# First block of a two-block transformer kernel: three feed-forward pieces kept for the last accumulation, the last transposes moved behind its first products, and ScalarE applying the next block's norm

## The chip, the cores and the metric

The kernel runs on one core of a Trainium2 chip. The metric is the device time of one execution in microseconds (us), the median of several runs; lower is better. TensorE (PE) multiplies matrices, VectorE (DVE) and ScalarE (ACT) work element by element, GpSimd (POOL) does small column arithmetic here, and SyncE (SP) issues the weight loads. Each engine works through its own instructions in their order and meets the others only at semaphores, so an instruction that waits holds up all that stand behind it on its engine.

## What is computed

256 rows of width 1024 pass through a first block of two layers and then a second block of two layers. The change touches the end of both layers of the first block and the first norm of the second. Cut to that part:

```python
for i in range(2):                                   # first block
    ...                                              # attention, gating, w_o, layer norm 1
    gate, up = jnp.split(x @ w_ffn_in[i], 2, axis=-1)          # 1024 -> 2 x 2816
    ffn = (jax.nn.silu(gate) * up) @ w_ffn_out[i]              # 2816 -> 1024
    ple = (p[i] @ w_ple[i]) * jax.nn.sigmoid(x @ w_ple_gate[i])
    x = layer_norm(ALPHA * x + ffn + ple, ln2_g[i], ln2_b[i])
for layer in range(2):                               # second block
    h = modulate(rms_norm(x, norm_mix[layer]), sh1, sc1)       # x*rsqrt(mean(x^2)+eps), then scale and shift
    ...                                              # h @ w_in, attention, w_out, squared-relu MLP
```

## The kernel before

The rows are two tiles of 128 (`t` is 0 or 1). Every float32 product is made of three: each operand is split in a high and a low part, and high x high, high x low and low x high are added up in PSUM. So a weight piece ("item", at most 128x2048) is loaded by SP into `RAW`, its high part written to `WB` by ACT (`high`, L1737; in the trace every activation has line L1732), and its low part by DVE (`low`, L1939). The activations are split likewise: `XTH`/`XTL` for x transposed, `HTH`/`HTL` for the feed-forward's middle.

The order of the work is written out by one Python pass: `do(part, ...)` appends to a list, and each engine's program then walks through that list. `advance` issues high and low parts for at most three items ahead of the products (`cur["pairs"]`); `plan` gives the order of the weights in memory, which is the order of loads and of use.

The feed-forward runs over 11 pieces of 256 columns. For piece `c` PE makes two items of `w_ffn_in` (24 products of 512 columns each), ACT applies silu (`ffn`, L1868), DVE multiplies into `GB` (L2268). `ffn_turn` transposes a piece on PE (4 products of 128 columns, L1631); ACT then writes `HTH` and DVE `HTL` (L2022). Only then can the piece be multiplied with its item of `w_ffn_out` (24 products, `partial`), which accumulates in four PSUM banks, one for each tile `t` and half `c` of the 1024 output columns. Pieces 0 to 8 are multiplied as soon as they are transposed. Pieces 9 and 10 are kept for one last call of `partial`, which goes bank by bank in the order (t,c) = (0,0), (0,1), (1,0), (1,1), so that the first rows can be finished while the last are still being multiplied.

`last` follows each bank: DVE adds it to `X` (L2276) and makes the statistics of half a row (L2229). After the second half of a tile come the aggregate (L2234), POOL's reciprocal root (`rsqrt`, L1527 and L1529), and DVE's `ln_scale` (L2240) and `ln_shift` (L2248), which leaves the layer's result in `X`. In layer 0 that tile is transposed straight into `XTH`/`XTL`. In layer 1 the second block's norm stands between: ACT squares and sums the row (`norm_sq`, L1884), POOL makes the root, DVE multiplies into `MIX` (`norm_apply`, L2253), PE transposes (`modulate`), ACT scales and shifts half the columns and writes `XTH`, DVE does the other half and `XTL` (L2040, L2046). `go(0, pad=14)` is the call that does this for tile 0; `pad` is a number of products without use (L1584) that PE makes ahead of the transposes.

Then `linear2` multiplies with `even_w_in_2`: for tile 0 the items 139 and 140 (128x1536 each), the transposes of tile 1, item 141 (128x1152), and then the same items for tile 1.

Of the kernel before, what the change touches and what calls it, by code (L numbers as in the profile page):

```python
# [13 lines left out]
ACT = mybir.ActivationFunctionType  # L14
# [32 lines left out]
def plan():  # L47
# [12 lines left out]
    for i in range(2):  # L60

        all_rows("w_in", i, 1024, (768, 1092), (1604, 2116), (0, 384), (384, 768), (1092, 1604))
        all_rows("w_ple", i, 256, halves[0])
        all_rows("w_o", i, 1024, *halves)
        all_rows("w_ple", i, 256, halves[1])
        all_rows("w_ple_gate", i, 1024, *halves)
        for c in range(12):
            if c < 11:
                all_rows("w_ffn_in", i, 1024, [(c * 256, c * 256 + 256), (DFF + c * 256, DFF + c * 256 + 256)])
            if 1 <= c <= 8:  # L70
                ada(*ADA[i * 8 + c - 1])
            if c:
                out.append(("w_ffn_out", i, (c * 256 - 256, c * 256), [(0, 1024)]))
    for i in range(2):
# [110 lines left out]
def program(nc, W, xd, xTd, pTd, posd, pos2d, colvd, cstd, cstbd, vecd, sgwd, smalld, condd, out):  # L185
    with ExitStack() as ctx:
# [83 lines left out]
        def do(part, *args):  # L270
            order.append((part, args))
# [3 lines left out]
        def take():  # L275
            return free.pop(0)
# [231 lines left out]

        def partial(name, parts, ps, first, last, evac=None):
            its = []  # L510
# [14 lines left out]
            if evac is None:  # L525
                for n in range(len(its)):
                    advance()
                    one(n, 0)
                    one(n, 1)
            else:  # L530
                assert len(its) <= cur["pairs"]
                advance()

                for t in range(2):
                    for c in range(2):
                        for n in range(len(its)):
                            one(n, t, (c,))
                        evac(t, c, ("mm", (g, t, c)))
                advance()
# [225 lines left out]

        def norm_sums(t, after):
            g = uid()
            ss = col(1)
            do("norm_sq", g, t, ss, after)
            do("rsqrt", ("nt", g), ss, 1.0 / D, 1e-6, ("norm_sq", g))  # L770

            def apply():
                do("norm_apply", g, t, ss)
                hn[t] = ("hn", g)
            return apply

        def norm_tile(t, after):
            norm_sums(t, after)()

# [20 lines left out]
        for i in range(2):  # L800
# [185 lines left out]
            ht_free = [list(t_pe), list(t_pe)]  # L986
            acc4 = None
            for c in range(12):
# [6 lines left out]
                if c:  # L995
                    d = c - 1
                    r2 = 2 * (d % 4)
                    b, fr = take()
                    g = uid()
                    do("ffn_turn", g, [GB[:, t, (d % 2) * 256 + kt * 128:(d % 2) * 256 + kt * 128 + 128]  # L1000
                                       for kt in range(2) for t in range(2)], r2, b,
                       [("ffn", (i, d, t)) for t in range(2)] + fr, ht_free[d % 2])
                    give(b, ("tl", g))
                    f_free[d % 2] = [("tp", g)]
                if c < 11:
                    run(gen)
                if c:
                    if acc4 is None:
                        acc4 = [[take(), take()], [take(), take()]]
                    part_ = (r2, [("tl", g)])  # L1010
                    if d < 9:
                        ht_free[d % 2] = [partial("w_ffn_out", [part_], acc4, d == 0, False)]
                    elif d == 9:
                        part9 = part_
            x_o, x_n = x_w, [None, None]
# [11 lines left out]
            def last(t, c, done):  # L1027
                do("add_out", (i, t, c), t, c, acc4[t][c][0], [done] + x_o[t])
                give(acc4[t][c][0], ("add_out", (i, t, c)))
                ln_half((i, 2, t), t, c, ("add_out", (i, t, c)))  # L1030
                if c == 0:
                    return

# [4 lines left out]

                before = norm_sums(0, x_n[0]) if t and i else None
                x_n[t] = ln_tile((i, 2, t), t, between, before, (lambda: go(0, pad=14)) if t and i else None)  # L1040
                if t and i:
                    advance(1)
                if t and i == 1:
                    norm_tile(1, x_n[1])

            t_pe = [partial("w_ffn_out", [part9, part_], acc4, False, True, last)]
            pt_free = list(t_pe)
# [681 lines left out]
        def scalar_program(eng):  # L1729
# [154 lines left out]
            def norm_sq(g, t, ss, after):  # L1884
                for e in after:
                    on.wait_ge(*at(*e))
                act(MIX[:, t, :], X[:, t, :], ACT.Square, accum_out=ss).then_inc(*up("norm_sq", g))

            def lambdas(lt, _):
                on.wait_ge(*at("lam_dot", 0))  # L1890
                act(lt, lt, ACT.Exp).then_inc(*up("lam_exp", 0))
# [24 lines left out]
            def diff_out(t, b, r, _, __, op, after):  # L1916
# [3 lines left out]
                for e in after:  # L1920
# [4 lines left out]
                         modulate=modulate, hin=hin, lat=lat, gelu=gelu, sel_score=sel_score, sgu_ln=sgu_ln,  # L1925
                         p_split=p_split, soft=soft, ple=ple, gate=gate, ffn=ffn, relu2=relu2, norm_sq=norm_sq,
                         lambdas=lambdas, lat_sq=lat_sq, mla_k=mla_k, qk_sq=qk_sq, gain=gain, diff_out=diff_out)
# [541 lines left out]
```

## Time and profile before

| | us |
|---|---|
| median of 3 runs | 1319.9 (1319.08 to 1319.96) |
| the profiled execution, its own time | 1320.38 |
| its span, first to last instruction | 1318.6 |
| PE busy | 1279.9 (97%) |
| DVE busy | 912.1 (69%) |
| ACT busy | 659.2 (50%) |
| POOL busy | 110.9 (8%) |
| mean granted clock of PE | 0.994 |

Times in the rows below are microseconds from the span's start, of that one profiled execution. The 3% in which PE is not busy is made of many waits of about one microsecond.

### The profile page before, as it was taken

What the parts mean: (1) busy time and instruction counts of PE and PEld (TensorE: products, weight loads), DVE (VectorE), ACT (ScalarE), POOL (GpSimd) and SP (SyncE); (2) the same over time, 40 slices, a digit from 0 to 9 for tenths busy, and PEclk for the clock granted to TensorE, in tenths of its full rate; (3) what the DMA queues carried; (4) which work ended last, traced back from release to release, by engine and by line L of the source; (5) the groups of instructions that cost most, each with busy time, mean ns of one, the idle gap of its engine ahead of it and who ended that gap; (6) DMA issues with size and microseconds to landing.
All of it is one profiled execution on the core that took longest, in us unless ns stands there. A gap on an engine that the chain in (4) does not pass through costs nothing.

```text
span 1318.6 us, 15858 instructions
## 1 busy us (share of the span) xinstructions
PE 1279.9 (97%) x6336; PEld 1058.8 (80%) x6336; DVE 912.1 (69%) x1223; ACT 659.2 (50%) x888; POOL 110.9 (8%) x145
## 2 busy tenths in 40 slices
PE   8999999999999999999999899999999979999998
PEld 6878888887878888888699787888887867888886
DVE  6968777766787777775768857857567775744444
ACT  6645433443563543344475646545446654745442
POOL 2002000000000100000225200000004320000000
PEclk9999999999999999999999999999999989999999
DMA  9616678873643678886264305876765420555450
GB/s 376 248 65 234 238 302 309 306 290 132 224 152 114 228 265 312 303 307 226 67 211 145 112 10 215 314 292 256 287 223 191 160 96 32 194 189 192 170 181 32
DMA packets 41113, 270.35 MB, mean 205 GB/s; under 512 B 4656, under 2 KB 4672, under 8 KB 12880
## 3 DMA queue, kind: packets, MB, share of 16 engines
q1 hardware_dynamic: 38288, 259.83, 53.4%
q0 software_dynamic: 2464, 8.98, 1.8%
q8 instruction: 50, 0.82, 0.2%
q10 hardware_dynamic: 288, 0.52, 0.1%
q14 instruction: 23, 0.19, 0.0%
HBM read 268.27 MB, written 1.05 MB: 204 GB/s over the span
## 4 chain that ended last, share of the span: by engine, by line
PE 79%; DVE 12%; ACT 5%; issue 2%; POOL 1%; DMA 0%; DVEq 0%; ACTq 0%; POOLq 0%
PE ps L1617 48%; PE ps L1607 24%; PE ps L1631 4%; DVE WB L1939 3%; PE ps L1719 2%; ACT WB L1732 1%; ACT E L1732 1%; DVE st L2155 1%; PE ps L1694 1%; DVE SCR L2057 1%; POOL st L1529 1%; DVE SCR L2058 1%; ACT XTH L1732 0%; DMA GB<-xTd 0%; DVE st L2308 0%
## 5 line engine op out<-in xcount | busy, mean ns | idle before, releaser
L1939 DVE TENSOR_TENSOR WB<-RAW,WB 128x2048 fp32r<-128x2048 f32 (+3 forms) x211 | 453.2, 2151 | 239.3 <-ACT WB L1732 238.9
L1732 ACT ACTIVATE WB<-RAW 128x2048 fp32r<-128x2048 f32 (+3 forms) x211 | 379.8, 1802 | 206.2 <-PE ps L1617 202.5
L1607 PE MATMUL ps<-WB,XTH 128*128 128x512 f32 (+3 forms) x1176 | 312.5, 387 | 6.2 <-ACT XTH L1732 4.1
L1617 PE MATMUL ps<-WB,XTH 128*128 128x512 f32 (+3 forms) x1176 | 304.6, 380 | 4.8 <-DVE WB L1939 4.7
L1617 PE MATMUL ps<-WB,XTL 128*128 128x512 f32 (+3 forms) x1176 | 303.9, 380 | 1.9 <-DVE XTL L2046 1.4
L1617 PEld LDWEIGHTS ps<-WB,XTH 128*128 128x128 f32 x1176 | 217.4, 189 | 47.1 <-DVE WB L1939 9.0
L1617 PEld LDWEIGHTS ps<-WB,XTL 128*128 128x128 f32 x1176 | 218.3, 189 | 41.3 <-DVE XTL L2046 2.3
L1607 PEld LDWEIGHTS ps<-WB,XTH 128*128 128x128 f32 x1176 | 212.8, 189 | 44.4 <-ACT XTH L1732 7.2
L1607 PE MATMUL ps<-WB,HTH 128*128 128x512 f32 (+1 forms) x452 | 126.9, 396 | 0.6 <-ACT HTH L1732 0.5
L1617 PE MATMUL ps<-WB,HTH 128*128 128x512 f32 (+1 forms) x452 | 126.5, 395 | 0.0
L1617 PE MATMUL ps<-WB,HTL 128*128 128x512 f32 (+1 forms) x452 | 126.4, 394 | 0.0
L2001 DVE CUSTOM_DVE_ANT_0 RAW<-RAW,cond,colv 128x1024 f32<-128x1024 f32 x96 | 119.3, 1280 | 0.0
L1527 POOL TENSOR_SCALAR st<-st 128x1 f32<-128x1 f32 (+2 forms) x40 | 27.5, 688 | 909.2 <-DVE st L2234 518.3
L1617 PEld LDWEIGHTS ps<-WB,HTH 128*128 128x128 f32 x452 | 84.9, 188 | 20.3
L1732 ACT ACTIVATE HTH<-ps 128x512 fp32r<-128x512 f32 (+1 forms) x58 | 32.0, 587 | 138.3 <-PE ps L1631 138.1
L1617 PEld LDWEIGHTS ps<-WB,HTL 128*128 128x128 f32 x452 | 85.0, 188 | 20.0
L1607 PEld LDWEIGHTS ps<-WB,HTH 128*128 128x128 f32 x452 | 84.6, 188 | 20.6 <-ACT HTH L1732 1.0
L1732 ACT ACTIVATE GB<-ps 128x256 f32<-128x256 f32 (+1 forms) x86 | 41.9, 488 | 91.9 <-PE ps L1617 91.9
L1732 ACT ACTIVATE E<-ps,st 128x128 f32<-128x128 f32 (+1 forms) x104 | 46.8, 458 | 66.7 <-DVE st L2171 38.9
L2022 DVE TENSOR_TENSOR HTL<-ps,HTH 128x512 fp32r<-128x512 f32 x54 | 35.7, 685 | 31.9 <-ACT HTH L1732 31.9
L1529 POOL TENSOR_TENSOR st<-st,cst 128x1 f32<-128x1 f32 (+2 forms) x40 | 51.1, 1278 | 3.3
L1732 ACT ACTIVATE H<-ps 128x384 f32<-128x384 f32 (+2 forms) x48 | 24.5, 534 | 26.8 <-PE ps L1617 26.5
(183 smaller groups left out, 948.8 us busy)
## 6 DMA issues: line engine op xcount, KB each, us to landing
RAW<-W SPq DMA_DIRECT2D x220, 1024.0 KB, 4.9
RAW<-W SPq DMA_DIRECT2D x22, 768.0 KB, 4.5
VEC<-vecd POOLq DMA_DIRECT2D x10, 512.0 KB, 5.6
RAW<-W SPq DMA_DIRECT2D x8, 512.0 KB, 3.6
RAW<-W SPq DMA_DIRECT2D x4, 576.0 KB, 3.8
RAW<-W SPq DMA_DIRECT2D x2, 648.0 KB, 3.9
T<-sgwd POOLq DMA_DIRECT2D x2, 512.0 KB, 8.5
X<-xd SPq DMA_DIRECT2D x1, 1024.0 KB, 18.5
```

Source lines behind the costliest of these rows:

```text
L1527: eng.tensor_scalar(x, x, scale, eps, ALU.mult, ALU.add).then_inc(*own.up())
L1529: eng.tensor_tensor(x, x, MH.to_broadcast([128, x.shape[1]]), ALU.pow).then_inc(*up("rsqrt", key))
L1607: eng.matmul(banks[b][:, 0:cw], x2[j][0], hi[:, j, c0:c0 + cw], start=first and j == 0, stop=False)
L1617: op = eng.matmul(banks[b][:, 0:cw], x2[j][0 if low_w else 1], (lo if low_w else hi)[:, j, c0:c0 + cw], start=False, stop=last and end and ...
L1631: op = eng.transpose(banks[b][0:rows, j * 128:j * 128 + 128], src, ident)
L1694: eng.matmul(banks[b][:, c:c + nk], q, ks, start=n == 0, stop=True, skip_group_check=True)
L1719: op = eng.matmul(banks[b][:, c0:c0 + dv], PET[:, u["i"], blk * 128:blk * 128 + 128], val, start=(j == 0), stop=(j == len(lst) - 1))
L1732: return eng.activation(dst, src, f, **k)
L1939: eng.tensor_tensor(WB[:, it["raw"], 0:w], RAW[:, it["raw"], 0:w], WB[:, it["high"], 0:w].bitcast(F32), ALU.subtract).then_inc(*up("wl", n))
L2001: op = eng.tensor_tensor_reduce(view[:, q, :], view[:, q, :], cond[:, :], 1.0, colv[:, b0:b0 + 1], ALU.mult, ALU.add, modc[:, it["layer"], ...
L2022: eng.tensor_tensor(HTL[:, r2:r2 + 2, :], banks[b][:, :].rearrange("p (n q) -> p n q", n=2), HTH[:, r2:r2 + 2, :].bitcast(F32), ALU.subtra ...
L2057: eng.tensor_tensor(P4, x4, cb, ALU.mult).then_inc(*own.up())
```

## The change

`plan` and the loop over the pieces now keep pieces 8, 9 and 10 for the last call of `partial`; piece 8 is no longer multiplied between the `w_ffn_in` items. Piece 10 is transposed inside that call, through `turn_last`, after piece 8's products for bank (0,0). For tile 1 piece 8's products are made for both halves first. In layer 1 the norm of both tiles is applied by ACT (`norm_apply_a`), tile 0's as soon as its layer norm is done; `go(0)` comes right behind the last bank with `pad=6`, and the layer norm of tile 1 comes behind it.

```diff
@@ plan
-            if c:
-                out.append(("w_ffn_out", i, (c * 256 - 256, c * 256), [(0, 1024)]))
+            for d in range(8 if c == 10 else c - 1, c) if c and c != 9 else ():
+                out.append(("w_ffn_out", i, (d * 256, d * 256 + 256), [(0, 1024)]))
@@ partial
                 for t in range(2):
                     for c in range(2):
                         for n in range(len(its)):
+                            if turn_last and t and n == 0:
+                                if c == 0:
+                                    one(0, 1)
+                                    advance(1)
+                                continue
                             one(n, t, (c,))
+                            if turn_last and (t, c, n) == (0, 0, 0):
+                                turn_last()
                         evac(t, c, ("mm", (g, t, c)))
@@ norm_sums(t, after, by="norm_apply"), norm_tile(t, after, by="norm_apply")
-                do("norm_apply", g, t, ss)
+                do(by, g, t, ss)
@@ the loop over the pieces
-                    if d < 9:
+                    if d < 8:
                         ht_free[d % 2] = [partial("w_ffn_out", [part_], acc4, d == 0, False)]
-                    elif d == 9:
-                        part9 = part_
+                    else:
+                        kept.append(part_)
@@ last
                 if c == 0:
+                    if t and i:
+                        norm_tile(0, x_n[0], "norm_apply_a")
                     return
...
-                before = norm_sums(0, x_n[0]) if t and i else None
-                x_n[t] = ln_tile((i, 2, t), t, between, before, (lambda: go(0, pad=14)) if t and i else None)
+                if t and i:
+                    go(0, pad=6)
+                x_n[t] = ln_tile((i, 2, t), t, between)
                 if t and i:
                     advance(1)
-                if t and i == 1:
-                    norm_tile(1, x_n[1])
-            t_pe = [partial("w_ffn_out", [part9, part_], acc4, False, True, last)]
+                    norm_tile(1, x_n[1], "norm_apply_a")
+            t_pe = [partial("w_ffn_out", kept, acc4, False, True, last, lambda d=d, r2=r2, g=g: turn_ffn(d, r2, g))]
@@ scalar_program
+            def norm_apply_a(g, t, ss):
+                on.wait_ge(*at("rsqrt", ("nt", g)))
+                act(MIX[:, t, :], X[:, t, :], ACT.Copy, scale=ss).then_inc(*up("hn", g))
```

What this does to the engines' orders, at three places. On PE, at the end of the loop over the pieces (either layer; `cst,GB` are the transposes, HTH and HTL the feed-forward's middle), there stood before:

```order
L1617 MATMUL ps<-WB,XTH 128x512 x4
L1631 MATMUL ps<-cst,GB 128x128 x4
L1607 MATMUL ps<-WB,HTH 128x512 x2
L1617 MATMUL ps<-WB,HTH 128x512 x2
L1617 MATMUL ps<-WB,HTL 128x512 x2
```

and now stands:

```order
L1632 MATMUL ps<-WB,XTH 128x512 x4
L1622 MATMUL ps<-WB,HTH 128x512 x2
L1632 MATMUL ps<-WB,HTH 128x512 x2
L1632 MATMUL ps<-WB,HTL 128x512 x2
L1646 MATMUL ps<-cst,GB 128x128 x4
L1622 MATMUL ps<-WB,HTH 128x512 x2
```

Six products of piece 8 now stand ahead of the transposes of piece 10; piece 9's follow, and piece 10's are the third six.

On ACT, in layer 1 from the last silu (`GB<-ps`) to the first norm, before:

```order
L1732 ACTIVATE WB<-RAW 128x2048
L1732 ACTIVATE GB<-ps 128x256 x2
L1732 ACTIVATE HTH<-ps 128x512
L1732 ACT_TABLE_LOAD
L1732 ACTIVATE st<-st 128x2
L1732 ACTIVATE WB<-RAW 128x1536
L1732 ACTIVATE MIX,st<-X 128x1024
L1732 ACTIVATE GB<-ps,modc 128x128 x4
```

and now:

```order
L1747 ACTIVATE GB<-ps 128x256 x2
L1747 ACT_TABLE_LOAD
L1747 ACTIVATE st<-st 128x2
L1747 ACTIVATE WB<-RAW 128x2048
L1747 ACTIVATE HTH<-ps 128x512
L1747 ACTIVATE WB<-RAW 128x1536
L1747 ACTIVATE MIX,st<-X 128x1024
L1747 ACTIVATE MIX<-X,st 128x1024
L1747 ACTIVATE GB<-ps,modc 128x128 x4
```

The high part of piece 10's weights (128x2048) moved behind the last silu, since three items are already ahead, and with the table load it stands ahead of `HTH`; layer 0 has the same order without the table load and the small exponential. The norm's multiplication (`MIX<-X,st`) is new on ACT.

On DVE, in layer 1 from the last bank's addition to `X`, before:

```order
L2276 TENSOR_TENSOR X<-X,ps 128x512
L2229 BN_STATS st<-X 128x6
L2234 BN_AGGR st<-st 128x2
L2253 TENSOR_SCALAR MIX<-X,st 128x1024
L2240 SCALAR_TENSOR_TENSOR X<-X,st,VEC 128x1024
L2040 TENSOR_SCALAR GB<-ps,modc 128x128 x4
L2046 TENSOR_TENSOR XTL<-GB,XTH 128x4x128 x2
L2248 SCALAR_TENSOR_TENSOR X<-X,st,VEC 128x1024
L1939 TENSOR_TENSOR WB<-RAW,WB 128x1536
```

and now:

```order
L2295 TENSOR_TENSOR X<-X,ps 128x512
L2248 BN_STATS st<-X 128x6
L2059 TENSOR_SCALAR GB<-ps,modc 128x128 x4
L2065 TENSOR_TENSOR XTL<-GB,XTH 128x4x128 x2
L2253 BN_AGGR st<-st 128x2
L2259 SCALAR_TENSOR_TENSOR X<-X,st,VEC 128x1024
L2267 SCALAR_TENSOR_TENSOR X<-X,st,VEC 128x1024
L1958 TENSOR_TENSOR WB<-RAW,WB 128x1536
```

Tile 0's modulation moved ahead of tile 1's aggregate and scale. Item 140's low part (128x1536) still stands behind tile 1's shift.

## Rows read from the trace of the kernel before

**Rows 1.** The page, busy time of an engine, share of the span, instructions:

```profile
PE 1279.9 (97%) x6336; PEld 1058.8 (80%) x6336; DVE 912.1 (69%) x1223; ACT 659.2 (50%) x888; POOL 110.9 (8%) x145
```

**Rows 2.** Waits of PE: us in total, times, longest us:

```profile
PE ps L1631 <- DVE GB L2268: 2.0, 2, 1.0
...
PE ps L1631 <- DVE X L2248: 1.3, 1, 1.3
```

**Rows 3.** Timeline, layer 1's last piece: start, us, engine, line [idle before <- releaser]:

```profile
623.13 1.91 ACT L1732 ACTIVATE WB<-RAW 128x2048 fp32r<-128x2048 f32 x1
...
625.08 2.29 DVE L1939 TENSOR_TENSOR WB<-RAW,WB 128x2048 fp32r<-128x2048 f32 x1 [1.11 <-ACT WB L1732]
...
627.02 1.07 PE L1617 MATMUL ps<-WB,XTH 128*128 128x512 f32 x4
...
628.13 0.38 ACT L1732 ACTIVATE GB<-ps 128x256 f32<-128x256 f32 x1 [2.33 <-PE ps L1617]
628.54 0.42 DVE L2268 TENSOR_TENSOR GB<-GB,ps 128x256 f32<-128x256 f32 x1 [0.84 <-ACT GB L1732]
...
629.11 0.63 PE L1631 MATMUL ps<-cst,GB 128*128 128x128 f32 x4 [1.02 <-DVE GB L2268]
...
629.49 0.71 PE L1607 MATMUL ps<-WB,HTH 128*128 128x512 f32 x2
629.77 0.60 ACT L1732 ACTIVATE HTH<-ps 128x512 fp32r<-128x512 f32 x1 [1.26 <-PE ps L1631]
...
630.39 1.28 ACT L1732 ACT_TABLE_LOAD   x1
630.40 0.69 DVE L2022 TENSOR_TENSOR HTL<-ps,HTH 128x512 fp32r<-128x512 f32 x1 [1.44 <-ACT HTH L1732]
```

**Rows 4.** Timeline, layer 1, tile 0's layer norm, norm and transposes:

```profile
636.30 0.67 DVE L2276 TENSOR_TENSOR X<-X,ps 128x512 f32<-128x512 f32 x1
...
638.05 1.28 DVE L2240 SCALAR_TENSOR_TENSOR X<-X,st,VEC 128x1024 f32<-128x1024 f32 x1
638.11 1.27 POOL L1527 TENSOR_SCALAR st<-st 128x1 f32<-128x1 f32 x1 [201.28 <-DVE st L2234]
...
640.06 1.28 DVE L2248 SCALAR_TENSOR_TENSOR X<-X,st,VEC 128x1024 f32<-128x1024 f32 x1 [0.73 <-POOL st L1529]
...
640.81 3.20 PE L1584 MATMUL ps<-cstb 128*128 128x512 bf16 x14
...
641.38 1.06 ACT L1732 ACTIVATE MIX<-X 128x1024 f32<-128x1024 f32 x1 [8.11 <-DVE X L2248]
...
642.62 0.19 POOL L1527 TENSOR_SCALAR st<-st 128x1 f32<-128x1 f32 x1 [2.59 <-ACT MIX L1732]
642.89 0.55 POOL L1529 TENSOR_TENSOR st<-st,cst 128x1 f32<-128x1 f32 x1
...
644.22 0.70 DVE L2253 TENSOR_SCALAR MIX<-X,st 128x1024 f32<-128x1024 f32 x1
...
644.98 1.09 PE L1631 MATMUL ps<-cst,MIX 128*128 128x128 f32 x8 [0.97 <-DVE MIX L2253]
```

**Rows 5.** Timeline, first products of the second block, tile 0, then tile 1:

```profile
647.87 1.29 DVE L2046 TENSOR_TENSOR XTL<-GB,XTH 128x512 fp32r<-128x512 f32 x2 [0.39 <-ACT XTH L1732]
...
647.89 1.05 PE L1607 MATMUL ps<-WB,XTH 128*128 128x384 f32 x4
...
650.28 1.75 DVE L1939 TENSOR_TENSOR WB<-RAW,WB 128x1536 fp32r<-128x1536 f32 x1
...
653.60 1.10 PE L1631 MATMUL ps<-cst,MIX 128*128 128x128 f32 x8
...
656.61 0.93 PE L1607 MATMUL ps<-WB,XTH 128*128 128x384 f32 x4 [0.32 <-ACT XTH L1732]
```

**Rows 6.** Timeline, layer 0, PE's transposes of tile 1:

```profile
332.98 1.07 PE L1631 MATMUL ps<-cst,X 128*128 128x128 f32 x8 [1.25 <-DVE X L2248]
```

**Rows 7.** Windows: length, busy us of PE, PEld, DVE, ACT, POOL, granted clock, DMA:

```profile
1080.80:1084.10 3.30, 1.35 (x14) 0.74 (x12) 2.89 (x8) 1.42 (x6) 1.01 (x1) 1.00 0.01 2
1084.30:1094.30 10.00, 8.81 (x29) 6.50 (x30) 8.52 (x12) 6.29 (x18) 0.00 (x0) 0.50 0.00 0
```

More of the change, by code:

```diff
@@ L507, in run, with partial @@
                 pass
-        def partial(name, parts, ps, first, last, evac=None):
+        def partial(name, parts, ps, first, last, evac=None, turn_last=None):
             its = []
@@ L764, in program, with norm_sums @@
         hn = [None, None]
-        def norm_sums(t, after):
+        def norm_sums(t, after, by="norm_apply"):
             g = uid()
@@ L772, in apply, with norm_tile @@
             def apply():
-                do("norm_apply", g, t, ss)
+                do(by, g, t, ss)
                 hn[t] = ("hn", g)
             return apply
-        def norm_tile(t, after):
-            norm_sums(t, after)()
+        def norm_tile(t, after, by="norm_apply"):
+            norm_sums(t, after, by)()
         def norm_mod(layer, k, after):
@@ L986, in program, with turn_ffn @@
             ht_free = [list(t_pe), list(t_pe)]
-            acc4 = None
+            acc4, kept = None, []
+            def turn_ffn(d, r2, g):
+                b, fr = take()
+                do("ffn_turn", g, [GB[:, t, (d % 2) * 256 + kt * 128:(d % 2) * 256 + kt * 128 + 128]
+                                   for kt in range(2) for t in range(2)], r2, b,
+                   [("ffn", (i, d, t)) for t in range(2)] + fr, ht_free[d % 2])
+                give(b, ("tl", g))
+                f_free[d % 2] = [("tp", g)]
             for c in range(12):
@@ L995, in program @@
                 if c:
[L996 to L1007, printed above, removed]
+                    d, r2, g = c - 1, 2 * ((c - 1) % 4), uid()
+                    if c < 11:
+                        turn_ffn(d, r2, g)
+                        run(gen)
                     if acc4 is None:
@@ L1010, in program @@
                     part_ = (r2, [("tl", g)])
-                    if d < 9:
+                    if d < 8:
                         ht_free[d % 2] = [partial("w_ffn_out", [part_], acc4, d == 0, False)]
-                    elif d == 9:
-                        part9 = part_
+                    else:
+                        kept.append(part_)
+                else:
+                    run(gen)
             x_o, x_n = x_w, [None, None]
@@ L1925, in scalar_program @@
                          modulate=modulate, hin=hin, lat=lat, gelu=gelu, sel_score=sel_score, sgu_ln=sgu_ln,
-                         p_split=p_split, soft=soft, ple=ple, gate=gate, ffn=ffn, relu2=relu2, norm_sq=norm_sq,
+                         p_split=p_split, soft=soft, ple=ple, gate=gate, ffn=ffn, relu2=relu2, norm_apply_a=norm_apply_a, norm_sq=norm_sq,
                          lambdas=lambdas, lat_sq=lat_sq, mla_k=mla_k, qk_sq=qk_sq, gain=gain, diff_out=diff_out)
```

## The prediction

> **What bounds the kernel.** The page comes first: PE is busy 97% of the span [rows 1], so only two things can save time, less work on PE or shorter waits of PE. The change removes no product. The waits of PE [rows 2] give the sizes: the two transposes of piece 10 wait for DVE's `GB`, 2.0 us in total and 1.0 each, and layer 0's transposes of tile 1 wait 1.3 for `X`. The timeline of layer 1 then shows three stretches: the end of the pieces [rows 3], tile 0's norm [rows 4], and the first products of the second block [rows 5]. I write P for the time at which PE is through with piece 10's `w_ffn_in` products, and E for the time at which it is through with the last bank. Before, in layer 1: the last four products start at 627.02 and take 0.9 of issue (48 products from 629.49 to 640.81 are 0.236 each), so P = 627.93 [rows 3]; E = 640.81 [rows 4]. From P to the transposes at 629.11 are 1.18 us, the stall that the change attacks, and it is the same in layer 0.
>
> **Part 1, the third piece kept.** The number of products is the same: 24 of piece 8 and 48 of the last call now make 72. Without stalls that is no gain and no loss; only their place moves.
>
> **Part 2, transposes behind six products.** Piece 8's six products take 6 x 0.236 = 1.42 us, more than the 1.18 of the stall, so the transposes find `GB` ready: 1.18 us less in each layer. What is late next is piece 10. Its products are the third six, which PE reaches at P + 1.42 + 0.38 (the transposes, 629.11 to 629.49) + 1.42 = P+3.2. They need four things: the high part of their weights, `HTH`, the low part, `HTL`. Before, high and low were made at 623.13 (ACT, 1.91) and 625.08 (DVE, 2.29), ahead of P [rows 3]. Three items may be ahead and now pieces 8, 9 and 10 all are in one call, so piece 10's high part waits for the last `w_ffn_in` item: the orders show it on ACT behind the last silu and ahead of `HTH`, and on DVE the low part ahead of `HTL`.
>
> Layer 0: the last silu ends at P+0.6 (628.13 + 0.38). High 1.91: P+2.45. `HTH` 0.60: P+3.0. Low 2.29 on DVE: P+4.75. `HTL` 0.69: P+5.45. PE starts the third six at P+3.2, makes two products (0.47), waits for the low part until P+4.8 (1.1), makes two, waits 0.2 for `HTL`: 1.3 us of new stall. Net +0.1.
>
> Layer 1: the table load (1.28) and a small exponential now come ahead of the high part, which ends at P+3.9; `HTH` P+4.35; low P+6.2; `HTL` P+6.9. PE waits 1.1 for `HTH`, 1.4 for the low part, 0.2 for `HTL`: 2.7 us. Net +1.55. Queued behind these on ACT is only item 139's high part, which waits for piece 8's buffer anyway.
>
> Bounds of this part: if the high part were ready as before, 0 of new stall, -2.4 us over both layers; if each wait were a product longer, +0.5 more.
>
> **Part 3, tile 0's norm in layer 1.** Bank (0,1) is finished three sixes' worth of two banks plus piece 8's, 36 products or 8.5 us, ahead of E; before it was 5.6. From the addition at 636.30 to the end of the shift (640.06 + 1.28) are 5.0 us [rows 4], so `X` is ready at E-3.3 (before E+0.5). `norm_sq` starts right away; POOL's root was ready 2.06 after its start (641.38 to 642.89 + 0.55). Here POOL meets item 139's low part on DVE, up to E-1.45, so take E-0.8. ACT's multiplication is not in the trace; its nearest row is the square of the same 1024 columns, 1.06 us, where DVE takes 0.70. That gives the norm at E+0.3, and the six products without use end at about E+1.3 (14 take 3.0): the transposes start at E+1.3 instead of E+4.17 (644.98). The first products of the second block follow 2.9 later (647.89 - 644.98), at E+4.2 instead of E+7.1.
>
> **Part 4, what tile 1 makes of it.** These 2.9 us are given back if PE waits for item 140's low part, which stands on DVE behind tile 1's shift. PE needs it after item 139 and two thirds of item 140, 3.7 us after the first product: E+7.9. DVE: tile 0's `XTL` ends 4.2 after the transposes began (647.87 + 1.29 - 644.98), E+5.5. Then the aggregate, scale, root and shift, 3.5 (0.2 ahead of 638.05, then to 641.34): `X` of tile 1 at E+9.0, where it was 650.28 - 640.81 = E+9.5. Low part 1.75: E+10.8. PE stalls from E+7.9 to E+10.8, 2.9 us, all of the lead. Meanwhile the norm of tile 1: `norm_sq` from E+9.05; POOL ready to start at E+10.3, but DVE's low part runs until E+10.8. The row for that is 638.11: the same POOL instruction that took 0.19 at 642.62 took 1.27 beside DVE's `ln_scale` (638.05 to 639.33), ending with it [rows 4]. Root at E+11.45, ACT's multiplication at E+12.5, transposes at E+12.6, where they were E+12.8 (653.60). Behind them item 141's high part now comes after ACT's multiplication, E+13.6, and its low part E+15.1. PE reaches tile 1's first product at E+15.7 instead of E+15.8 (656.61) [rows 5]. Gain 0.1. Bounds: 0 at one end; 2.9 at the other, if neither item 140 nor the norm of tile 1 were in the way.
>
> The POOL lock is what the Trainium skill's page "SBUF — State Buffer", section "Who interferes with whom", speaks against this change with: GpSimd and a VectorE instruction with two SBUF inputs exclude each other for a whole instruction. By it tile 1's root is late; with POOL free it would come at E+11.2, ACT would end at E+12.3, and item 141's path would set the rest, 0.2 us better. The row at 638.11 agrees with the page.
>
> **Layer 0 behind E.** Tile 0's `X` is early, and DVE has item 70's low part behind it, so tile 1's aggregate comes some 0.9 sooner; but item 72's low part, which needs ACT until about E+4.7, still stands ahead of tile 1's scale. `X` of tile 1 comes at about E+9.7 instead of E+10.0, so PE's wait at 332.98 [rows 6] hides the rest. Gain 0.2; with the +0.1 above: about 0.
>
> **Part 5, the clock.** The granted clock is full in these stretches now. But in the window 1080.8 to 1084.1 PE was busy 1.35 us of 3.3, and in 1084.3 to 1094.3 it was granted half, the lower level of 1.2 GHz instead of 2.4 [rows 7]. The new stall of 2.9 us at E+7.9, and the group of 2.7 us of waits in 3.6 in layer 1, are as bare. After the first about 3.4 us of PE work follow (rest of item 140, fillers, transposes, item 141), which at half rate take twice that, less about 1.2 of waits that lie there anyway: at most +2.2, at least 0. After the second, the products that follow set E: at most some +2 again. Whether the clock falls depends on how the stall lies; I take +0.9 for both, between the ends.
>
> **The sum.** Layer 0: 0. Layer 1: +1.55 - 0.1 = +1.45. Clock: +0.9. Together +2.35 on the profiled execution, 1320.4 to 1322.7; its own time is 0.5 above the median, so the median goes from 1319.9 to 1322.2.
>
> **The rivals.**
> - *Stalls as above, the clock stays full*: +1.45, 1321.3. For it: PE's longest waits at these places were 1.0 and 1.3 [rows 2], and six products without use still stand at E. Against it: the window of rows 7.
> - *The clock falls at both places for long*: +1.45 + 2 + 2, 1324 to 1325.5.
> - *Faster*: tile 0's lead is not given back. Place: DVE behind the last bank. If tile 1's shift and item 140's low part end by E+7.9, and tile 1's norm follows, up to 2.9 are kept, and with 2.4 of stalls removed and no new ones the kernel comes to 1314.7. It decides at 3 us earlier on DVE than I add up. Against it: each instruction's place in the order is fixed.
> - *It does nothing*: the new stalls are just the old 1.18 in another place, 1319.9. That is nearly so in layer 0; in layer 1 the table load and the 128x2048 high part speak against it, 3.2 us of ACT ahead of `HTH`.
> - *A shift of the timeline changes how the low-clock stretch at 1077 to 1094 falls*: a stretch as long as 1080.8 to 1084.1 more or less at half rate is some 1.7 us, either sign.
>
> **How the numbers follow.** A stall in layer 1 with some loss of clock (1321.8 to 1323.5) 0.32; full clock (about 1321.3) 0.24; both places for long, 0.17; nothing, or small gains down to 1317.5, 0.14; faster beyond that 0.13. The first is the likeliest: 1322.2, its own range 1321 to 1323.8. The range over the cases is 1317 to 1325.5: it leaves out the farther half of the faster case and the end of the slow one. The bound of 0.2%, what a measurement of this kernel tells from no change, is 2.6 us: faster (under 1317.3) 0.14, same (to 1322.5) 0.48, slower 0.38.
>
> **What would show it.** In the changed trace: (1) the `cst,GB` transposes of piece 10 without a wait; (2) right after, L1632 `WB,HTH` waiting for DVE `WB` over 1 us in both layers, and in layer 1 L1622 `WB,HTH` for ACT `HTH`; (3) `MIX` transposes 1.3 us behind the last bank; (4) L1632 of 128x384 waiting 2 to 3 us for DVE `WB`; (5) the granted clock below 1.00 between the last bank and tile 1's transposes, or not. If (2) or (4) is absent I am wrong towards faster. What could make all of it wrong is a buffer or load that comes later than before: the order of loads on SP is unchanged.

## The result, and the profile after

The changed kernel takes 1321.47 us against 1319.12 before, medians of 20 runs each. The ratio is 1.0018, 95% interval [1.0012, 1.0024], so it is slower by 1.6 to 3.2 us; 1322.2 from 1319.9 was forecast, 2.3 up. The step is met; the time itself is 0.7 under the forecast, since the kernel before has 1319.12 in 20 runs and had 1319.9 in the three that the forecast started from. The profiled executions alone would say less: 1321.44 against 1320.38 of their own time, spans of 1319.6 and 1318.6. Where the other 1.3 us are is shown below the table of stretches. Single executions that took far longer (one of 2431 us in norm_alone and one of 3252 us in early_local, among others) are left out of all medians and ratios.

The page, busy time by engine, as [rows 1]:

```profile
PE 1279.5 (97%) x6328; PEld 1058.3 (80%) x6328; DVE 911.2 (69%) x1221; ACT 662.1 (50%) x890; POOL 109.5 (8%) x145
```

PE is as busy as before, to 0.4 us. The waits of PE, as [rows 2] (us in total, times, longest):

```profile
PE ps L1632 <- DVE WB L1958: 9.0, 8, 2.6
...
PE ps L1622 <- ACT HTH L1747: 1.5, 3, 1.0
PE ps L1646 <- DVE X L2267: 1.5, 1, 1.5
```

The two waits for `GB` are gone from the list. The wait for the low part `WB` is now 9.0 us, where before it was 4.7 in 6 waits, longest 1.1; `HTH` went from 0.5 to 1.5. Timeline of layer 1's end, as [rows 3]:

```profile
622.20 0.62 PE L1622 MATMUL ps<-WB,HTH 128*128 128x512 f32 x2
...
622.40 0.39 ACT L1747 ACTIVATE GB<-ps 128x256 f32<-128x256 f32 x1 [2.34 <-PE ps L1632]
...
622.81 1.28 ACT L1747 ACT_TABLE_LOAD   x1
...
623.60 0.60 PE L1646 MATMUL ps<-cst,GB 128*128 128x128 f32 x4
...
624.21 1.90 ACT L1747 ACTIVATE WB<-RAW 128x2048 fp32r<-128x2048 f32 x1
...
626.01 0.57 ACT L1747 ACTIVATE HTH<-ps 128x512 fp32r<-128x512 f32 x1
626.14 2.29 DVE L1958 TENSOR_TENSOR WB<-RAW,WB 128x2048 fp32r<-128x2048 f32 x1 [1.25 <-ACT WB L1747]
...
626.64 0.73 PE L1622 MATMUL ps<-WB,HTH 128*128 128x512 f32 x2 [1.03 <-ACT HTH L1747]
628.35 0.68 DVE L2041 TENSOR_TENSOR HTL<-ps,HTH 128x512 fp32r<-128x512 f32 x1
...
628.49 0.74 PE L1632 MATMUL ps<-WB,HTH 128*128 128x512 f32 x2 [1.11 <-DVE WB L1958]
```

PE begins its six products of piece 8 at 622.20; that is P. The `cst,GB` transposes follow at 623.60 without a wait. On ACT the table load and the high part stand between the silu and `HTH`, on DVE the low part between `GB` and `HTL`, and PE stands idle twice, before 626.64 and before 628.49. Then the norm of tile 0, as [rows 4], and the first products of tile 0 and tile 1, as [rows 5]:

```profile
641.52 1.15 ACT L1747 ACTIVATE MIX<-X,st 128x1024 f32<-128x1024 f32 x1 [1.20 <-POOL st L1544]
...
642.32 1.47 PE L1599 MATMUL ps<-cstb 128*128 128x512 bf16 x6
...
643.62 1.04 PE L1646 MATMUL ps<-cst,MIX 128*128 128x128 f32 x8
...
646.46 1.29 DVE L2065 TENSOR_TENSOR XTL<-GB,XTH 128x512 fp32r<-128x512 f32 x2 [0.40 <-ACT XTH L1747]
...
646.48 1.03 PE L1622 MATMUL ps<-WB,XTH 128*128 128x384 f32 x4
...
647.91 1.28 DVE L2259 SCALAR_TENSOR_TENSOR X<-X,st,VEC 128x1024 f32<-128x1024 f32 x1
...
649.91 1.28 DVE L2267 SCALAR_TENSOR_TENSOR X<-X,st,VEC 128x1024 f32<-128x1024 f32 x1 [0.72 <-POOL st L1544]
651.12 1.75 DVE L1958 TENSOR_TENSOR WB<-RAW,WB 128x1536 fp32r<-128x1536 f32 x1
...
652.47 0.45 POOL L1542 TENSOR_SCALAR st<-st 128x1 f32<-128x1 f32 x1 [2.59 <-ACT MIX L1747]
...
652.92 0.96 PE L1632 MATMUL ps<-WB,XTH 128*128 128x384 f32 x4 [2.63 <-DVE WB L1958]
...
654.79 1.93 PE L1646 MATMUL ps<-cst,MIX 128*128 128x128 f32 x8 [0.45 <-ACT MIX L1747]
...
658.91 0.86 PE L1622 MATMUL ps<-WB,XTH 128*128 128x384 f32 x4
```

The transposes of tile 0 begin 1.30 behind the last bank (E = 642.32), where they began 4.17 behind it. Item 140's low part still stands behind tile 1's shift: it starts at 651.12, and PE waits 2.63 us for it. The transposes of tile 1 take 1.93 for what took 1.10. The windows show why (length, busy PE, granted clock, DMA share, GB/s):

```profile
650.30:652.90 2.60, 0.00 (x0) 1.00 0.00 0
652.90:654.80 1.90, 1.43 (x7) 1.00 0.00 0
654.80:658.40 3.60, 3.60 (x17) 0.53 0.00 0
658.40:668.00 9.60, 9.60 (x66) 1.00 0.51 160
```

PE made nothing for 2.60 us, and soon after it had begun again it was granted 0.53 over 654.8 to 658.4: the lower level, 1.2 GHz instead of 2.4, for most of it.

**Stretches.** Since a start-up that differs by some tenths moves every later row, all traces are compared between seven marks on PE: M, its wait for `T` near 62; E0, layer 0's transposes of tile 0; B, the product near 396 that waits 0.41 for `XTH`; E, the first product without use behind layer 1's last bank; T1, tile 1's first product of the second block; S, the `cst,E` transposes near 1074 that wait for DVE; F, the product near 1105 that waits 0.15 for `XTH`. The first row is in us and the others are differences to it, but the last column is in us in every row; from F to the end all take 213.3 to 213.4 us. In three traces (fill_stall, lam_late, la2_before) the record of the first product without use is missing, and E is set 0.23 earlier, one such product.

| | M to E0 | E0 to B | B to E | E to T1 | sum of the four | T1 to S | S to F (us) |
|---|---|---|---|---|---|---|---|
| before (us) | 260.48 | 73.13 | 244.80 | 15.80 | 594.21 | 417.06 | 31.52 |
| changed | -0.01 | -0.37 | +1.57 | +0.79 | +1.98 | +0.01 | 30.31 |
| ff_alone | +0.01 | -0.42 | +1.51 | -1.18 | -0.08 | +0.11 | 28.52 |
| norm_alone | -0.02 | -0.04 | -0.06 | +2.47 | +2.35 | +0.11 | 28.47 |
| scale_first | -0.01 | -0.34 | +1.57 | -1.91 | -0.69 | 0.00 | 31.58 |
| lam_late | +0.01 | -0.37 | +0.05 | +0.45 | +0.14 | -0.08 | 30.04 |
| fill_stall | +0.04 | -0.36 | +3.06 | -0.14 | +2.60 | +0.03 | 31.48 |
| dve_tile1 | -0.01 | -0.37 | +3.14 | -0.67 | +2.09 | +0.08 | 31.46 |
| early_local_look | -1.29 | -0.39 | -1.22 | +0.63 | -2.27 | +0.09 | 30.18 |
| early_high | -1.38 | -1.88 | -1.26 | +0.38 | -4.14 | -0.05 | 30.04 |
| la2_before | -0.12 | -1.58 | -0.07 | -0.01 | -1.78 | -0.02 | 29.37 |
| early_scale | -1.35 | -1.86 | -1.27 | -1.91 | -6.39 | +0.08 | 30.23 |
| early_scale_dve | -1.35 | -1.95 | -1.28 | -2.43 | -7.01 | +0.07 | 30.24 |

The changed kernel's trace has +1.98 in the four stretches that the change can reach. From S to F, which begins 417 us behind T1, PE has the same products in all kernels, but the thirteen traces spread over 28.47 to 31.58 us, with half clock granted in more or less of it [rows 7]. The profiled execution of before was near the long end and that of the changed kernel 1.2 below it: that hides most of the loss in the profiled pair. The medians of 20 runs, 2.35 apart, show no sign of it.

### The profile page after: what moved, and what is told of

Same layout as the page of the kernel before. It is cut to its first block, busy times and chain, and to the rows that moved or that the text cites. A ratio compares the mean times of both kernels' runs of the same rounds, so it can differ in the third digit from the quotient of the medians.

```text
span 1319.6 us, 15842 instructions
## 1 busy us (share of the span) xinstructions
PE 1279.5 (97%) x6328; PEld 1058.3 (80%) x6328; DVE 911.2 (69%) x1221; ACT 662.1 (50%) x890; POOL 109.5 (8%) x145
## 3 DMA queue, kind: packets, MB, share of 16 engines
HBM read 268.27 MB, written 1.05 MB: 204 GB/s over the span
## 4 chain that ended last, share of the span: by engine, by line
PE 80%; DVE 11%; ACT 5%; issue 2%; POOL 1%; DMA 0%; ACTq 0%; DVEq 0%; POOLq 0%
PE ps L1632 48%; PE ps L1622 24%; PE ps L1646 4%; DVE WB L1958 4%; ACT WB L1747 2%; PE ps L1734 1%; ACT E L1747 1%; DVE st L2174 1%; PE ps L1709 1%; DVE SCR L2076 1%; DVE SCR L2077 1%; POOL st L1544 0%; DMA GB<-xTd 0%; ACT XTH L1747 0%; DVE st L2327 0%
```

## The experiments

Each edit is made to the changed kernel, if not said otherwise; the lines with - and + are the edit, and ... stands for lines left out. The ratio stands against runs of before on the same chip.

**ff_alone**: only the feed-forward's part of the change.

```diff
-                    if t and i:
-                        norm_tile(0, x_n[0], "norm_apply_a")
-                if t and i:
-                    go(0, pad=6)
-                x_n[t] = ln_tile((i, 2, t), t, between)
+                before = norm_sums(0, x_n[0]) if t and i else None
+                x_n[t] = ln_tile((i, 2, t), t, between, before, (lambda: go(0, pad=14)) if t and i else None)
...
-                    norm_tile(1, x_n[1], "norm_apply_a")
+                if t and i == 1:
+                    norm_tile(1, x_n[1])
```

> The changed kernel with only its feed-forward part (three pieces kept, the last transposes behind six products); the second block's norm as before: DVE multiplies, 14 products without use, ln_scale of tile 1 ahead of tile 0's modulation. My theory: the last bank of layer 1 ends 1.5 us later than before (642.3), since piece 10's high part waits for the last silu; from there tile 0's transposes come at +3.2, tile 1's first product of the second block at +14.9 (657.2, 0.6 later than before), without a half clock. In all +0.6 us to before. Rival (the lost time belongs to the feed-forward part as a whole, and the norm's part is neutral): +2.3, as the full change.

Measured: 1319.45 us, ratio 1.0004 [0.9994, 1.0014]. B to E is 1.51 longer, as forecast; E to T1 gives 1.18 of it back (0.9 forecast), and T1 is at 656.66 (657.2). So the feed-forward's part is no loss by itself, although its stall is there in full: the four stretches sum to -0.08. Nearly all of the +1.98 of the full change comes with the norm's part, which turns E to T1 from -1.18 into +0.79.

**norm_alone**: only the norm's part; this is the changed kernel with plan, loop and `partial` of before.

```diff
-            for d in range(8 if c == 10 else c - 1, c) if c and c != 9 else ():
-                out.append(("w_ffn_out", i, (d * 256, d * 256 + 256), [(0, 1024)]))
+            if c:
+                out.append(("w_ffn_out", i, (c * 256 - 256, c * 256), [(0, 1024)]))
...
+                    turn_ffn(d, r2, g)
                     if c < 11:
-                        turn_ffn(d, r2, g)
...
-                    if d < 8:
+                    if d < 9:
...
-            t_pe = [partial("w_ffn_out", kept, acc4, False, True, last, lambda d=d, r2=r2, g=g: turn_ffn(d, r2, g))]
+            t_pe = [partial("w_ffn_out", kept, acc4, False, True, last)]
```

> The kernel before with only the norm's part of the change (ScalarE multiplies, 6 products without use, tile 0's modulation ahead of tile 1's layer norm); pieces and transposes as before. My theory: the last bank ends as before (640.8); tile 0's norm is ready 4.0 behind it, so its lead is only 0.2, while tile 1's X comes at about +11.7 instead of +9.5 and item 140's low part at +13.5: a wait of nearly 3 us on DVE's WB, and tile 1's first product 2.4 us later than before, 3.5 with a half clock. Rival (the norm's part is the good half and the weights are the bad one): 1 us or more faster than before.

Measured: 1321.81 us (median of seven), ratio 1.0029 [1.0018, 1.0039]. E to T1 is 2.47 longer. The forecast had 2.4 with a full clock and 3.5 with a half one. The clock did fall, but at another place and behind another wait, so that 2.47 meets 2.4 is partly luck. From the timeline:

```profile
644.85 1.09 PE L1646 MATMUL ps<-cst,MIX 128*128 128x128 f32 x8 [2.39 <-ACT MIX L1747]
645.77 4.01 PE L1599 MATMUL ps<-cstb 128*128 128x512 bf16 x10
649.29 1.19 PE L1622 MATMUL ps<-WB,XTH 128*128 128x384 f32 x4
...
654.19 0.97 PE L1632 MATMUL ps<-WB,XTH 128*128 128x384 f32 x4 [0.93 <-DVE WB L1958]
...
656.05 1.09 PE L1646 MATMUL ps<-cst,MIX 128*128 128x128 f32 x8 [0.45 <-ACT MIX L1747]
```

With only two pieces kept the norm is ready 3.9 behind the bank (E = 640.98), and six products without use leave PE waiting 2.39 us. The next ten products without use then take 4.01 us instead of 2.32, with 0.50 granted from 647 to 649, and push tile 0's first products some 1.5 us back. So the wait for `WB` is 0.93 instead of nearly 3: PE is late itself.

**scale_first**: tile 1's aggregate and scale ahead of tile 0's modulation on DVE.

```diff
-                if t and i:
-                    go(0, pad=6)
-                x_n[t] = ln_tile((i, 2, t), t, between)
+                x_n[t] = ln_tile((i, 2, t), t, between, None, (lambda: go(0, pad=6)) if t and i else None)
```

> The changed kernel, but tile 1's aggregate and ln_scale stand ahead of tile 0's modulation on DVE, as before the change (ln_shift behind it). My theory: layer 1's last bank stays at 642.3; tile 0's modulation is 0.75 us later, tile 1's shift 1.4 us earlier, the wait for item 140's low part falls from 2.6 to about 0.5 us, the clock stays full, and tile 1's first product comes at +14.2 (656.5 instead of 658.9). In all 2.4 us faster than the changed kernel, level with before. Rival (the wait is set by ACT's high part or by the norm of tile 1, not by DVE's order): under 1 us faster than the changed kernel.

```profile
645.20 1.04 PE L1644 MATMUL ps<-cst,MIX 128*128 128x128 f32 x8
...
648.06 1.03 PE L1620 MATMUL ps<-WB,XTH 128*128 128x384 f32 x4
...
652.73 0.96 PE L1630 MATMUL ps<-WB,XTH 128*128 128x384 f32 x4 [0.49 <-DVE WB L1956]
...
654.60 1.09 PE L1644 MATMUL ps<-cst,MIX 128*128 128x128 f32 x8 [0.46 <-ACT MIX L1745]
...
657.79 0.95 PE L1620 MATMUL ps<-WB,XTH 128*128 128x384 f32 x4
```

Measured: 1320.16 us, ratio 1.0006 [0.9997, 1.0014]. The wait is 0.49, the transposes of tile 1 take 1.09, and T1 stands 13.89 behind E (14.2 forecast). The stretch is 2.7 shorter than the changed kernel's; of that 1.6 us appear in the ratios (1.0018 to 1.0006), whose intervals overlap. The order on DVE sets the wait, not ACT's high part.

**lam_late**: layer 1's table load and small exponential behind the last turn.

```diff
-                do("lambdas", col(2), list(scr["free"]))
-                scr["free"] = [("lam_dot", 0)]
...
+            def lam_exp_():
+                if i:
+                    do("lambdas", col(2), list(scr["free"]))
+                    scr["free"] = [("lam_dot", 0)]
...
-            t_pe = [partial("w_ffn_out", kept, acc4, False, True, last, lambda d=d, r2=r2, g=g: turn_ffn(d, r2, g))]
+            t_pe = [partial("w_ffn_out", kept, acc4, False, True, last, lambda d=d, r2=r2, g=g: (turn_ffn(d, r2, g), lam_exp_()))]
```

> The changed kernel, but layer 1's table load and small exponential on ScalarE (and their small vector work) stand behind the turn of the last piece instead of ahead of piece 10's high part. My theory: HTH comes 1.4 us earlier, the wait for ACT HTH (1.0) goes, the wait for DVE WB stays near 1, and the last bank comes 1.4 us earlier after the same start: layer 1's end costs 0.1 to 0.2 instead of 1.57 against before. In all 1.4 us faster than the changed kernel. Rival (HTH and the low part wait for something else, as the buffer of the weights): no change.

Measured: 1320.1 us, ratio 1.0008 [0.9999, 1.0017]. B to E is 0.05 longer than before instead of 1.57 (0.1 to 0.2 forecast). Layer 1's end then costs no more than layer 0's, and the table load (1.28 us) with the small exponential behind it (0.20) is the whole difference between them.

**early_high**: piece 10's weights made ahead of the last silu. For this the planner has four items ahead and loads one ahead around the last `w_ffn_in` piece. The edit did more than that: it also set the load-ahead of the whole program to two, where it is three.

```diff
-               "lag": False}
+               "lag": False, "la": 2}
...
-            while cur["load"] < len(seq) and most and cur["load"] - cur["item"] < NBUF - 2 * cur["pairs"] and bufs:
+            while cur["load"] < len(seq) and most and cur["load"] - cur["item"] < cur["la"] and bufs:
...
+                    if c == 10 and i in (0, 1):
+                        cur["la"], cur["pairs"] = 1, 4
...
+                        if c == 10:
+                            cur["la"], cur["pairs"] = 2, 3
```

> The changed kernel, but around the last w_ffn_in piece of each layer four items may be ahead and one weight is loaded ahead instead of two, so that piece 10's high and low parts are made before the last silu again. My theory: the new stalls behind the transposes go (1.3 us in layer 0, 2.7 in layer 1), so the last bank of layer 1 ends near 638.2 instead of 642.3; the wait for item 140's low part stays at 2.6 us and the clock still halves. In all 4.0 us faster than the changed kernel, 1.7 faster than before. Rival (the stall only moves again, to the next load or buffer, since a weight is loaded later): the same time as the changed kernel, or slower.

Measured: 1315.37 us, ratio 0.9972 [0.9961, 0.9983], and the last bank at 636.72: 1.5 us more than the theory had, in the stretch E0 to B, of which it said nothing. Two runs take the edits apart.

**early_local**, and **early_local_look**, one more execution of the same kernel, whose trace is read here: the load-ahead stays three (`"la": 3`), is two from the last `w_ffn_in` piece's start to its end, with four items ahead.

```diff
+                    if c == 10:
+                        cur["la"] = 2
+                    if c == 10:
+                        cur["pairs"] = 4
...
+                        if c == 10:
+                            cur["la"], cur["pairs"] = 3, 3
```

> The run early_high had two edits in one: besides the early high part, its planner kept two weights loaded ahead in the whole program where the kernels have three. Here the load-ahead is three as in the changed kernel everywhere, and only around the last w_ffn_in piece of each layer it is two with four items ahead. My theory: the early high part alone takes 1.4 us out of layer 0's end and 2.8 out of layer 1's end against the changed kernel (last bank at about 638.2 where the changed kernel has 642.3 and early_high 636.7), 4.2 in all. Rival (the gain of early_high was the load-ahead): 1.5 or less against the changed kernel.

> The kernel of early_local once more, since that run's profiled execution can't be read. By the theory: 1.4 us less than the changed kernel from layer 0's first products to its first transposes, 2.8 less at layer 1's end, no waits for HTH or WB behind the last cst,GB transposes; by the rival the waits are still there. The stretch behind layer 0's last bank, where early_high gained 1.5, stays as in the changed kernel if the load-ahead is its cause.

Measured: early_local 1317.3 us (median of ten), ratio 0.9986 [0.9977, 0.9995]; early_local_look 1317.04 us, one execution. From its timeline:

```profile
616.03 1.91 ACT L1753 ACTIVATE WB<-RAW 128x2048 fp32r<-128x2048 f32 x1
...
622.22 0.60 PE L1652 MATMUL ps<-cst,GB 128*128 128x128 f32 x4
...
622.86 0.60 ACT L1753 ACTIVATE HTH<-ps 128x512 fp32r<-128x512 f32 x1
...
623.49 0.69 DVE L2047 TENSOR_TENSOR HTL<-ps,HTH 128x512 fp32r<-128x512 f32 x1
```

The high part is made at 616.03, `HTH` right behind the transposes, and PE waits nowhere up to E, at 638.12 (638.2 forecast). Layer 0's end is 1.28 shorter than in the changed kernel, layer 1's 2.79 (1.4 and 2.8 forecast); E0 to B stays as in the changed kernel. That is the mechanism of part 2, with each term in its place.

**la2_before**: the kernel before with the load-ahead of two (the first two pieces of early_high's edit).

> The kernel before with one edit: two weights are loaded ahead of their high part instead of three, so a high part finds a free buffer earlier. My theory from the trace of early_high: ScalarE's high part behind layer 0's second tile starts 3 us earlier and PE's two waits for MIX of 0.55 go, 1.1 to 1.5 us faster than before. Rival (a transfer that starts later is late for its high part somewhere else): the same time or slower.

Measured: 1318.0 us, ratio 0.9993 [0.9984, 1.0001]. The trace shows -1.58 from E0 to B, where early_high had 1.51 beyond the changed kernel; the ratio alone doesn't settle a gain. ACT's high part behind layer 0's last bank, in la2_before and then in the changed kernel:

```profile
334.54 1.92 ACT L1732 ACTIVATE WB<-RAW 128x2048 fp32r<-128x2048 f32 x1
```

```profile
336.47 1.91 ACT L1747 ACTIVATE WB<-RAW 128x2048 fp32r<-128x2048 f32 x1 [1.77 <-PE ps L1632]
```

With three loads ahead nearly all nine buffers are taken and the high part waits for PE to free one (1.77 us behind PE's products); with two it doesn't, and PE's two waits of 0.56 for `MIX`, which DVE copies behind that item's low part, go.

**fill_stall**: eleven products without use on PE ahead of tile 0's item 140.

```diff
+                    if t == 0 and it is ia[1] and name == "even_w_in_2":
+                        do("fill", ps[1][0][0], ps[1][0][1], 11)
...
+            def fill(b, fr, n):
+                for e in fr:
+                    on.wait_ge(*at(*e))
+                busy(b, n)
```

> The changed kernel with eleven products without use (2.3 us) on PE ahead of tile 0's item 140, so that PE is busy where it waited 2.63 us for that item's low part; the order of DVE and ACT is untouched. My theory: the low part comes at the same time, PE waits only some 0.3 us, and the granted clock stays full: transposes of tile 1 and item 141 run at full rate, and tile 1's first product comes at +15.5 behind the last bank instead of +16.6, 1.1 us faster than the changed kernel. Rival (the half clock has another cause than the bare stall, or the fillers push back what PE does next): no change or slower, and the clock falls as before.

```profile
650.28 2.55 PE L1601 MATMUL ps<-cstb 128*128 128x512 bf16 x11
...
652.65 1.75 DVE L1965 TENSOR_TENSOR WB<-RAW,WB 128x1536 fp32r<-128x1536 f32 x1
...
654.45 0.96 PE L1639 MATMUL ps<-WB,XTH 128*128 128x384 f32 x4 [0.23 <-DVE WB L1965]
...
656.31 1.10 PE L1653 MATMUL ps<-cst,MIX 128*128 128x128 f32 x8 [0.45 <-ACT MIX L1754]
```

```profile
629.60:633.05 3.45, 3.45 (x10) 0.51 0.02 5
650.20:654.40 4.20, 4.02 (x21) 1.00 0.00 0
654.40:660.00 5.60, 4.86 (x28) 1.00 0.00 0
```

Measured: 1321.9 us, ratio 1.0020 [1.0011, 1.0029], no gain in the total. Behind E the trace is as the theory had it: a wait of 0.23, full clock, and T1 at E+15.66, 0.93 less than in the changed kernel. But the first window shows 0.51 granted in 629.6 to 633.05, right behind the two new waits at layer 1's end, where the changed kernel's trace has 1.00. These waits are the same 1.0 and 1.1 in both. B to E is 1.5 us longer for it. So this run doesn't show that the bare wait is what halves the clock behind E: the clock had already fallen and risen 20 us earlier.

**dve_tile1**: VectorE multiplies tile 1's norm.

```diff
-                    norm_tile(1, x_n[1], "norm_apply_a")
+                    norm_tile(1, x_n[1])
```

> The changed kernel with VectorE multiplying tile 1's norm, as before the change. It tells what ScalarE's multiplication is worth by itself. My theory: 0.3 to 0.5 us faster than the changed kernel between the last bank and tile 1's first product; the wait for item 140's low part and the half clock stay. Rival (ScalarE's multiplication is what the norm's part gains by): slower than the changed kernel by 0.5 or more.

```profile
654.60 0.97 PE L1632 MATMUL ps<-WB,XTH 128*128 128x384 f32 x4 [2.63 <-DVE WB L1958]
...
656.12 1.09 PE L1646 MATMUL ps<-cst,MIX 128*128 128x128 f32 x8
...
659.13 0.94 PE L1622 MATMUL ps<-WB,XTH 128*128 128x384 f32 x4 [0.33 <-ACT XTH L1747]
```

Measured: 1321.13 us, ratio 1.0016 [1.0007, 1.0024]. E to T1 is 1.46 shorter than in the changed kernel: the clock stayed full here (the transposes take 1.09) although the wait of 2.63 is as bare as before. Behind 0.93 for the clock about 0.5 remain for the multiplication, as forecast; but the half clock came at layer 1's end, as in fill_stall. Against the changed kernel the ratios don't tell these two apart.

**early_scale** joins the edits of early_high and scale_first; **early_scale_dve** adds that of dve_tile1. Both thus have two loads ahead in the whole program.

> early_high and scale_first together: the changed kernel with two weights loaded ahead, four items ahead around the last w_ffn_in piece, and tile 1's aggregate and ln_scale ahead of tile 0's modulation. My theory: the parts lie at different places and add up, so against before the stretches read in the two runs give -1.4 at layer 0's end, -1.9 behind it, -1.3 at layer 1's end and -1.9 from the last bank to tile 1's first product: 6.4 us faster than before, 2.3 faster than early_high. Rival (what the norm gains is eaten by a later high part or load, as PE arrives 4 us earlier): no better than early_high.

> early_scale with VectorE multiplying tile 1's norm, as before the change; ScalarE still does tile 0's. My theory: 0.80 on DVE instead of 1.15 on ACT, and item 141's high part no longer stands behind it: tile 1's transposes 0.3 to 0.4 us earlier, 6.8 us faster than before. Rival (DVE is the engine that is late there, so that a multiplication on it delays item 141's low part): 0.5 us slower than early_scale.

Measured: 1313.37 us, ratio 0.9958 [0.9946, 0.9970], and 1312.45 us, ratio 0.9946 [0.9933, 0.9959]. The stretches add up as forecast, -6.39 (-6.4) and -7.01 (-6.8). All waits of PE in early_scale_dve from 614 to 652 us, so from ahead of layer 1's last silu to behind T1 (649.80):

```profile
PE ps L1634 <- DVE WB L1960: 0.5, 1, 0.5
PE ps L1624 <- ACT XTH L1749: 0.3, 1, 0.3
```

Two waits, 0.8 us in all, are left in these 38 us. This kernel beats the changed one by some 9.5 us and the one before by 5.4 to 8.8.

## Why the prediction was right, point by point

- **Part 2, layer 1.** `HTH` ended at P+4.38 (4.35 forecast; the forecast's own terms, 3.9 and 0.60, give 4.5, but `HTH` starts 0.10 before the high part's recorded end), the low part at P+6.23 (6.2). Net +1.57 (+1.55). early_local_look and lam_late show the cause: take the high part ahead of the last silu, and all of the new stall goes; move the table load, and layer 1 costs what layer 0 does.
- **Part 2, layer 0.** Low part at P+4.70 (4.75), PE's wait for it 0.89 (1.1); the net is -0.01 (+0.1).
- **Part 3.** The norm was ready at E+0.35 (0.3), the transposes began at E+1.30 (1.3), the first products at E+4.16 (4.2).
- **Part 4.** PE needed the low part at E+7.97 (7.9) and had it at E+10.55 (10.8): 2.63 of wait (2.9). Tile 1's transposes began at E+12.47 (12.6). The lead of 2.9 is given back, and scale_first shows that DVE's order does it. Tile 1's gain without the clock is 0.14 (0.1), by the changed kernel's +0.79 less 0.93, and by fill_stall's -0.14.
- **The lock.** POOL's first instruction for tile 1's root started at 652.47 and took 0.45 us where the same one took 0.19 for tile 0 in the kernel before [rows 4]; it ended at 652.92, within 0.05 us of DVE's low part, and the root came after it, as part 4 had it; the trace agrees with the Trainium skill's page "SBUF — State Buffer", section "Who interferes with whom". No run took the lock away, so its 0.2 us stay a reading.
- **Layer 0 behind E.** -0.37 where a gain of 0.2 was forecast.
- **The clock.** +0.9 was taken for two places together. In the changed kernel's trace the first place, the wait of 2.63 us behind E, cost 0.93: from tile 1's transposes to T1 are 4.12 us, and 3.19 in scale_first, 3.20 in fill_stall. At the second place, the two waits at layer 1's end, it cost nothing in this trace and 1.5 in two of the five traces with both waits. The term was taken between two bounds and not from a row. That one place alone cost 0.93 in this trace, and the other nothing, is luck.

The sum of the waits alone was set too high by 0.4 (+1.05 measured as 1.98 - 0.93, where +1.45 stood), and all of it lies in layer 0 (-0.38 where 0 stood); layer 1 gave +1.43 for +1.45. So the mechanism is shown, but that the medians are 2.35 apart where 2.35 was forecast is partly luck: the trace has 1.98. The rest may be the clock at the second place in some of the runs, as the mean granted clock of the 20 runs is 0.9933, and 0.9959 in 25 runs of before; which stretch holds the difference isn't shown. The last rival, that the stretch at 1077 to 1094 falls otherwise, did happen between the two profiled executions (-1.2).

What stays open: with the wait of 2.63 us in place the clock fell in four of five traces (changed, lam_late, early_high, early_local_look; not dve_tile1), and behind the two waits at layer 1's end in two of five (fill_stall, dve_tile1; not changed, ff_alone, scale_first). In the two traces with a half clock at layer 1's end none came behind E. Whether that is more than chance, and whether the filler in fill_stall kept the clock or the earlier fall did, these traces don't tell. Between 600 and 670 us the clock fell in no trace where these waits were absent: seven traces at the first place, eight at the second. norm_alone is apart: it fell there behind a wait of its own, 2.39. Each of these seven stretches of half clock lasted 3.4 us (654.88 to 658.29 in the changed kernel's trace), and it cost 0.93 behind E in the changed kernel, where PE would have waited for other engines at full clock too, and 1.5 at layer 1's end, where PE's products follow each other without a wait.

## What to carry to other kernels

When products are kept back to cover a transposition, count the weight buffers they hold: here the stall of 1.18 us came back as 1.2 and 2.7 (net -0.01 and +1.57), since with three items already ahead the next weights' high part moved behind the last silu. With four items ahead (early_local_look) it was gone. A lead that one tile gains is worth only what the next instruction in order on the busiest helper engine lets through, so that order has to be moved along with the lead (2.7 us from E to T1 in scale_first, 0.93 of it the clock). Compare traces stretch by stretch between marks: the profiled executions here differ by 3 us in a stretch where PE has the same products in all.

## What was not expected of the hardware

The same products from S to F took 28.47 to 31.58 us. The granted clock went with it in part: from 1060 to 1110 it was 0.97 on average in ff_alone and 0.86 in the kernel before, but also 0.86 in the changed kernel, which took 1.2 us less than before. The same two waits of 1.0 and 1.1 us were followed by half clock in two traces and by full clock in three, at a cost of 1.5 us. And a shorter look-ahead of loads, two weights for three, was no loss anywhere in the trace and took 1.58 us from one place, since buffers and not transfers were short there.
